# Two stages of a long single-core kernel reordered: the S5 state loop and the pair loop of the sparse attention

## The chip, the cores and the metric

One core of one Trainium2 chip runs the whole program. The time is the device time in microseconds (us); the kernel before took 1408.51 us (median of 3 runs, 1407.64 to 1408.97).

## The reference

The program computes two blocks of a transformer-like network for 256 tokens and width 1024, in float32. The first has two layers of a hybrid mixer and a cross attention. The second has two layers, each a SwiGLU, a mixer and another SwiGLU. The mixer of its first layer is S5, that of its second is sparse attention. Only these two are touched here. Cut to what matters:

```python
def _s5_mixer(u, ...):                     # 64 groups of 16 channels, 64 complex states each
    bu_re, bu_im = einsum(ug, bb_re), einsum(ug, bb_im)
    x_re, x_im = associative_scan(combine, (la_re, la_im, bu_re, bu_im))   # x_t = a x_{t-1} + bu_t
    y = einsum(x_re, c_re) - einsum(x_im, c_im) + d_skip * ug
    y = gelu(y); return y * sigmoid(y @ w_glu)

def _nsa_mixer(u, kv, w_qg, q_norm, w_o, rel_bias):     # 16 heads, 4 key groups
    o_cmp = compressed branch (15 blocks of keys), o_slc = selected branch, o_win = window branch
    # at 256 tokens every block is selected, so slc and win are two dense causal softmaxes
    o = gates[..., 0:1] * o_cmp + gates[..., 1:2] * o_slc + gates[..., 2:3] * o_win
    return o.reshape(bsz, seq, D_MODEL) @ w_o
```

## The kernel before, in words

Nearly all the work is matrix products of weights that are streamed from memory once. Each unit of weights (128 x 1024) is loaded by SP into one of six slots (`RING = 6`), split by ACT into a high part (`hi_parts`, L332) and by DVE into a low part (`lo_parts`, L340), and TensorE (PE) then runs three products per tile (L392 to L394). Each engine follows one list written out by hand, and engines wait for each other by named semaphore values (`when(label)`). PSUM's eight banks go round in three pools, A (0 to 3), S (4, 5) and T (6, 7).

**The S5 core** (`pe_s5` L2281, `act_s5` L2375, `dve_s5` L2454, `pool_s5` L1967, `sp_s5` L2544) handles 1024 channels in eight groups q. The tokens are first rearranged by 32 transfers inside SBUF (`move_u`, 16 for each half a), issued by SP, ACT and POOL. Then, for each q:
- PE `drive(q)`: 32 small products (L2308) that give the input of the scan; `direct(q)`: 4 products (L2328) that start the output bank.
- DVE `products(q)`: two multiplications from PSUM (L2482), an addition and a subtraction (L2490, L2491), two scans (L2497), and one scaling `scale_u4(q+4)` (L2469) while q is below 4.
- POOL multiplies the scanned state by cosines (`s5.p{q}.0`) and sines (`s5.p{q}.1`, both L2063) and subtracts one from the other (`s5.x{q}`, L2066). For q = 7 DVE does this (`dve_last_state`, L2079 and L2082).
- PE multiplies three results into the output bank, 4 products each (L2340), and marks `s5.y{q}`. ACT copies the bank (L2411), PE turns it (`y_turn`, L2318), ACT applies GELU and makes the high part (`act_y`, L2364, L2367), DVE makes the low part (`dve_y_lo`, L2087), and PE turns two groups back for later (`pe_y_nat`, L2357).

The weights `glu` follow. Their units 0 to 3 go into slots that the S5 core uses until late: SP waits for `s5.direct3`, `s5.p6.1`, `s5.direct7` and `s5.p7.1` before it loads units 0, 2, 1 and 3.

**The pair loop** of the sparse attention takes 16 pairs p: two blocks of 128 queries, and in each eight pairs of heads. Pairs 0 to 7 have 128 keys, pairs 8 to 15 have 256. Each pair is two jobs j = 2p and 2p+1 (selected and window branch). The steps of a pair:
- PE scores (L2866) into both banks of pool S; DVE adds the bias and takes the maximum (L2901), which frees the banks; ACT exponentials with sums (L2912); DVE reciprocal (`dve_pair_sum`, L2928); POOL multiplies gate and probabilities (L2937, L2940);
- PE turns the probabilities (`pe_pair_turn`, L2877, pool T); ACT or DVE copies them back (`pair_copy`, L2923; `copied_by_act(j)` says who); PE multiplies with the values (L2887), one pair later.

The scores run `PAIRS_AHEAD = 2` pairs ahead of the turns. Other steps are put between pairs by the dictionaries `between`: conversions of the next weights (L332, L340) and the compressed branch: scores on PE (L3010), bias, maximum and subtraction on DVE (L3142, L3146, L3148), exponential on ACT (L3073), sum, reciprocal, gate and scaling on DVE (L3159 to L3165), turn (L3020) and product (L3032) on PE.

Of the kernel before, what the change touches and what calls it, by code (L numbers as in the profile page):

```python
# [16 lines left out]
P = 128  # L17
# [104 lines left out]
def build(nc, book, d, out, bias_rows):  # L122
    ctx = ExitStack()
    done, when = book.done, book.when
    with ctx:
# [1841 lines left out]
        def pool_s5(pool):  # L1967
# [81 lines left out]
            move_u(pool, 1, U_MOVES[12:16], "s5v")  # L2049
            pool.wait_ge(*when("s5.bu1"))  # L2050
            for q in (0, 1, 3):
                nc.gpsimd.memset(by_sin[q][:, 0, :, 0:1], 0.0).then_inc(*done("s5_pool", f"s5.s0{q}"))
            for q in range(KT - 1):
# [5 lines left out]
                if q == 3:  # L2059
                    pool.wait_ge(*when("s5.bu3"))  # L2060
                for i, (o, tab) in enumerate(((c, s5_cos), (s, s5_sin))):
                    w = bc(tab[:, q].rearrange("p (a c) -> p a c", a=4)[:, :, 0:NC4 - 1], 1, 2)
                    nc.gpsimd.tensor_tensor(o[:, :, :, 1:NC4], z, w, ALU.mult).then_inc(*done("s5_pool", f"s5.p{q}.{i}"))  # L2063
                pool.wait_ge(*when(f"s5.p{q}.0"))
                pool.wait_ge(*when(f"s5.p{q}.1"))
                nc.gpsimd.tensor_tensor(c[:, 0, :, 1:NC4], c[:, 0, :, 1:NC4], s[:, 1, :, 1:NC4], ALU.subtract  # L2066
                                        ).then_inc(*done("s5_pool", f"s5.x{q}"))
            pool.wait_ge(*when(f"s5.x{KT - 1}"))

        def dve_last_state(dve):  # L2070
# [9 lines left out]
            dve.wait_ge(*when(f"s5.p{q}.0"))  # L2080
            dve.wait_ge(*when(f"s5.p{q}.1"))
            nc.vector.tensor_tensor(c[:, 0, :, 1:NC4], c[:, 0, :, 1:NC4], s[:, 1, :, 1:NC4], ALU.subtract  # L2082
                                    ).then_inc(*done("s5_dve", f"s5.x{q}"))
# [197 lines left out]
        def pe_s5(pe):  # L2281
# [42 lines left out]
            for q in range(KT):  # L2324
                b = ahead if q == 1 else take(pe, "A", f"s5.yb{q}")
# [4 lines left out]
                last.then_inc(*done("s5_pe", f"s5.direct{q}"))  # L2330
                if q + 2 < KT:
# [15 lines left out]
            y_turn(KT - 1)  # L2347
            pe_chunk(pe, "glu.0", lifted="s5", after={7: lambda: pe_y_nat(pe, 3)})
# [26 lines left out]
        def act_s5(act):  # L2375
# [27 lines left out]
            move_u(act, 1, U_MOVES[4:12])  # L2403
            sines(3)
            for q in range(KT):
                if q == KT - 1:
# [7 lines left out]
                if q >= 4 and q % 2 == 0:  # L2414
                    act_y_nat(act, q // 2 - 2)
            hi_parts(act, chunk_start("glu.0") + 3)
            act_y(act, KT - 1)
# [36 lines left out]
        def dve_s5(dve):  # L2454
# [32 lines left out]
            for q in range(KT):  # L2487
# [46 lines left out]
        U_DONE = ((16 * 7, 16 * 9), (16 * 12, 16 * 4))  # L2534
# [65 lines left out]
        def pool_kv(pool):  # L2600
# [5 lines left out]
            pool.wait_ge(*when(f"s5.x{KT - 1}"))  # L2606
# [720 lines left out]
```

## Time and profile before

| | |
|---|---|
| median of 3 runs | 1408.51 us |
| the profiled execution | 1408.01 us |
| its span | 1406.0 us |
| PE busy | 1359.8 us (97%) |
| DVE busy | 831.9 us (59%) |
| ACT busy | 797.1 us (57%) |
| POOL busy | 341.8 us (24%) |

The span is from the first to the last instruction of the profile; the execution's own time is 2.01 us longer. Matmuls overlap each other, so PE counts as busy even where a product takes long. In the two stages that are changed PE is not always busy, and these are some 35 us (the S5 core) and 64 us (the pair loop) of the span.

### The profile page before, as it was taken

The page shows a single profiled execution, that of the slowest core. Times are in us where ns is not written, and L with a number is a line of the kernel's source. Part 1 is how long each engine was busy: PE and PEld are TensorE (multiplying, and loading weights), DVE is VectorE, ACT ScalarE, POOL GpSimd, SP SyncE. Part 2 cuts the span into 40 slices and gives each one's busy share as a digit, 9 for nine tenths or more (in the row PEclk, how much of TensorE's full clock was granted, in tenths as well). Part 3 has the DMA queues.
Part 4 walks back from the last instruction along what each step waited for, and adds up shares of the span by engine and source line. Part 5 has one row for each costly group of instructions (what it writes and reads, how often), then busy time and mean ns, then how long its engine had stood idle before and what let it go on. Part 6 is the DMA issues. An engine that isn't in the chain of part 4 may idle for free.

```text
span 1406.0 us, 22406 instructions
## 1 busy us (share of the span) xinstructions
PE 1359.8 (97%) x7511; PEld 1130.2 (80%) x7511; DVE 831.9 (59%) x1344; ACT 797.1 (57%) x1318; POOL 341.8 (24%) x398
## 2 busy tenths in 40 slices
PE   7999999999999999989999999999999978999998
PEld 6888878898777888868788888888888856888887
DVE  6547665457667566657755555645555686555553
ACT  7768476585665454555744445765444566554442
POOL 2011000013349999968200000010000045000000
PEclk9999999999999999999999999999999999999999
DMA  9541635631567554324866664686565401476561
GB/s 336 192 134 42 229 111 160 187 102 45 193 135 225 180 164 153 103 61 139 263 212 182 191 193 145 187 167 221 181 191 185 137 31 46 135 225 193 180 194 45
DMA packets 170863, 224.75 MB, mean 160 GB/s; under 512 B 14864, under 2 KB 114272, under 8 KB 170784
## 3 DMA queue, kind: packets, MB, share of 16 engines
q1 hardware_dynamic: 167888, 217.18, 49.2%
q0 software_dynamic: 2320, 6.18, 2.5%
q8 instruction: 48, 0.79, 0.2%
q10 hardware_dynamic: 576, 0.35, 0.1%
q14 instruction: 31, 0.25, 0.1%
HBM read 221.16 MB, written 1.44 MB: 158 GB/s over the span
## 4 chain that ended last, share of the span: by engine, by line
PE 47%; DVE 3%; ACT 2%; POOL 2%; issue 1%; DMA 1%; ACTq 0%; POOLq 0%; SPq 0%; DVEq 0%
PE psum L1638 12%; PE psum L1626 9%; PE psum L1628 8%; PE psum L1627 8%; PE psum L392 2%; PE psum L394 2%; PE psum L393 2%; PE psum L1665 1%; ACT w_hi L332 1%; DVE w_lo L340 1%; PE psum L2684 1%; POOL arena L2063 1%; DVE arena L2901 1%; PE psum L418 1%; PE psum L2877 0%
## 5 line engine op out<-in xcount | busy, mean ns | idle before, releaser
L1844 DVE TENSOR_TENSOR w_lo<-w_raw,w_hi 128x1024 fp32r<-128x1024 f32 x216 | 281.0, 1304 | 273.4 <-ACT w_hi L1764 273.1
L1764 ACT ACTIVATE w_hi<-w_raw 128x1024 fp32r<-128x1024 f32 x216 | 228.7, 1060 | 306.7 <-PE psum L1628 217.2
L340 DVE TENSOR_TENSOR w_lo<-w_raw,w_hi 128x1024 fp32r<-128x1024 f32 (+5 forms) x191 | 230.1, 1230 | 118.2 <-ACT w_hi L332 117.0
L1626 PE MATMUL psum<-w_hi,x_hi 128*128 128x512 f32 x704 | 280.1, 398 | 1.3 <-ACT arena L2770 0.5
L1628 PE MATMUL psum<-w_hi,x_lo 128*128 128x512 f32 x704 | 274.9, 390 | 0.0
L1627 PE MATMUL psum<-w_lo,x_hi 128*128 128x512 f32 x704 | 274.2, 389 | 0.0
L332 ACT ACTIVATE w_hi<-w_raw 128x1024 fp32r<-128x1024 f32 (+5 forms) x191 | 192.7, 1038 | 99.8 <-PE psum L394 56.7
L392 PE MATMUL psum<-w_hi,x_hi 128*128 128x512 f32 (+6 forms) x608 | 230.3, 379 | 2.1 <-DVE w_lo L340 1.4
L394 PE MATMUL psum<-w_hi,x_lo 128*128 128x512 f32 (+6 forms) x608 | 225.5, 371 | 0.0
L393 PE MATMUL psum<-w_lo,x_hi 128*128 128x512 f32 (+6 forms) x608 | 225.1, 370 | 0.0
L1626 PEld LDWEIGHTS psum<-w_hi,x_hi 128*128 128x128 f32 x704 | 132.3, 188 | 28.6 <-issue 1.5
L1628 PEld LDWEIGHTS psum<-w_hi,x_lo 128*128 128x128 f32 x704 | 132.1, 188 | 28.4
L1627 PEld LDWEIGHTS psum<-w_lo,x_hi 128*128 128x128 f32 x704 | 132.4, 188 | 25.8
L392 PEld LDWEIGHTS psum<-w_hi,x_hi 128*128 128x128 f32 x608 | 114.3, 188 | 22.0 <-DVE w_lo L340 1.4
L394 PEld LDWEIGHTS psum<-w_hi,x_lo 128*128 128x128 f32 x608 | 114.3, 188 | 19.4
L393 PEld LDWEIGHTS psum<-w_lo,x_hi 128*128 128x128 f32 x608 | 114.4, 188 | 17.4
L1638 PE MATMUL psum<-w_hi,f_hi 128*128 128x512 f32 x320 | 99.8, 393 | 1.2 <-DVE f_lo L1838 1.2
L1638 PE MATMUL psum<-w_lo,f_hi 128*128 128x512 f32 x320 | 98.6, 389 | 0.0
L1638 PE MATMUL psum<-w_hi,f_lo 128*128 128x512 f32 x320 | 98.6, 389 | 0.0
L1638 PEld LDWEIGHTS psum<-w_hi,f_lo 128*128 128x128 f32 x320 | 60.1, 188 | 12.6
L1638 PEld LDWEIGHTS psum<-w_lo,f_hi 128*128 128x128 f32 x320 | 60.1, 188 | 12.6
L1638 PEld LDWEIGHTS psum<-w_hi,f_hi 128*128 128x128 f32 x320 | 59.0, 188 | 13.3 <-issue 1.8
(436 smaller groups left out, 1712.0 us busy)
## 6 DMA issues: line engine op xcount, KB each, us to landing
w_raw<-in_ffn_w_in SPq DMA_DIRECT2D x352, 256.0 KB, 3.2
w_raw<-in_ffn_w_out SPq DMA_DIRECT2D x176, 256.0 KB, 2.9
w_raw<-in_w_in SPq DMA_DIRECT2D x88, 256.0 KB, 3.4
w_raw<-in_w_out SPq DMA_DIRECT2D x32, 256.0 KB, 3.7
w_raw<-in_w_kv SPq DMA_DIRECT2D x24, 256.0 KB, 2.9
w_raw<-in_mem_wk SPq DMA_DIRECT2D x16, 256.0 KB, 5.1
w_raw<-in_mem_wv SPq DMA_DIRECT2D x16, 256.0 KB, 5.1
w_raw<-in_mem_wq SPq DMA_DIRECT2D x16, 256.0 KB, 6.3
```

Of the source, the lines that this page charges most:

```text
L332: nc.scalar.activation(w_hi[:, s, 0:size(u)], w_raw[:, s, 0:size(u)], ACT.Copy).then_inc(hi_ready, 1)
L340: nc.vector.tensor_tensor(w_lo[:, s, 0:size(u)], w_raw[:, s, 0:size(u)], w_hi[:, s, 0:size(u)].bitcast(F32), ALU.subtract).then_inc(lo_rea ...
L392: nc.tensor.matmul(o, xh, whi, start=(k + i == x_first), stop=False)
L393: nc.tensor.matmul(o, xh, wlo, start=False, stop=False)
L394: last = nc.tensor.matmul(o, xl, whi, start=False, stop=(k + i == x_first + kts - 1))
L418: last = nc.tensor.transpose(psum[:, b, (2 * c + t) * P:(2 * c + t + 1) * P], src(t, 2 * f + c), ident[:])
L1626: nc.tensor.matmul(o, xh, whi, start=(kt == 0), stop=False)
L1627: nc.tensor.matmul(o, xh, wlo, start=False, stop=False)
L1628: last = nc.tensor.matmul(o, xl, whi, start=False, stop=(kt == KT - 1))
L1638: last = nc.tensor.matmul(psum[:, FF_ACC[2 * t + n], :], x, w[:, n * 512:(n + 1) * 512], start=(first and w is whi and x is xh), stop=Fals ...
L1764: nc.scalar.activation(w_hi[:, s, :], w_raw[:, s, :], ACT.Copy).then_inc(hi_ready, 1)
L1844: nc.vector.tensor_tensor(w_lo[:, s, :], w_raw[:, s, :], w_hi[:, s, :].bitcast(F32), ALU.subtract).then_inc(lo_ready, 1)
```

## The change

In S5:
- the second half's transfers are split 5, 5 and 6 between SP, ACT and POOL instead of 4, 8 and 4, and SP loads glu units 4 and 5 only when all transfers have landed;
- the subtraction `s5.x{q}` is gone. ACT negates the sine product's imaginary part (`s5.n{q}`), and PE multiplies four results into the bank, not three;
- `direct(q+1)` is issued in group q, ahead of that group's state products;
- on DVE the scalings of the second half move one group later (q = 1 to 4), and `dve_y_lo` runs twice in each of groups 5 and 6 instead of once in each of groups 4 and 5;
- the last `y_turn` moves into the first glu chunk, after two of its eight steps; ACT's order of `hi_parts` and `act_y(7)` changes with it.

In the pair loop:
- `PAIRS_AHEAD` is 3;
- the compressed scores are issued as two halves of 64 columns of weights, and one pair earlier (2 and 3 instead of 3 and 4);
- the compressed subtraction and the last scaling go to POOL, between jobs;
- conversions and compressed steps have other places in DVE's and ACT's lists, and ACT copies more of the turned jobs.

```diff
-            for q in (0, 1, 3):
-                nc.gpsimd.memset(by_sin[q][:, 0, :, 0:1], 0.0).then_inc(*done("s5_pool", f"s5.s0{q}"))
+            for q in range(2):
+                nc.gpsimd.memset(by_sin[q][:, :, :, 0:1], 0.0).then_inc(*done("s5_pool", f"s5.s0{q}"))
...
-                pool.wait_ge(*when(f"s5.p{q}.0"))
-                pool.wait_ge(*when(f"s5.p{q}.1"))
-                nc.gpsimd.tensor_tensor(c[:, 0, :, 1:NC4], c[:, 0, :, 1:NC4], s[:, 1, :, 1:NC4], ALU.subtract
-                                        ).then_inc(*done("s5_pool", f"s5.x{q}"))
-            pool.wait_ge(*when(f"s5.x{KT - 1}"))
+            pool.wait_ge(*when(f"s5.p{KT - 1}.1"))
...
+            ahead = direct(0)
+            for q in range(KT):
+                y = ahead
                 if q + 2 < KT:
                     drive(q + 2)
-                if q == 0:
-                    ahead = take(pe, "A", "s5.yb1")
-                    pe_busy(pe, ahead, 4)
-                for label, x, i in ((f"s5.p{q}.0", by_cos[q % 2][:, 1], 1), (f"s5.p{q}.1", by_sin[q][:, 0], 1),
-                                    (f"s5.x{q}", by_cos[q % 2][:, 0], 0)):
-                    pe.wait_ge(*when(label))
+                if q + 1 < KT:
+                    ahead = direct(q + 1)
+                c, s = by_cos[q % 2], by_sin[q]
+                for label, x, i in ((f"s5.p{q}.0", c[:, 1], 1), (None, c[:, 0], 0), (f"s5.p{q}.1", s[:, 0], 1), (f"s5.n{q}", s[:, 1], 0)):
+                    if label:
+                        pe.wait_ge(*when(label))
                     for j in BY_HALF:
                         last = nc.tensor.matmul(y[j // 2][:, :, j % 2, :], x[:, j, :], s5_D[:, 4 * q + j, i, :],
-                                                start=False, stop=(i == 0), skip_group_check=True)
+                                                start=False, stop=(label == f"s5.n{q}"), skip_group_check=True)
                 last.then_inc(*done("s5_pe", f"s5.y{q}"))
                 if q >= 1:
                     y_turn(q - 1)
                 if q % 2 and q >= 3:
                     pe_y_nat(pe, q // 2 - 1)
-            y_turn(KT - 1)
-            pe_chunk(pe, "glu.0", lifted="s5", after={7: lambda: pe_y_nat(pe, 3)})
+            pe_chunk(pe, "glu.0", lifted="s5", after={2: lambda: y_turn(KT - 1), 7: lambda: pe_y_nat(pe, 3)})
...
-            move_u(act, 1, U_MOVES[4:12])
+            move_u(act, 1, U_MOVES[5:10])
             sines(3)
             for q in range(KT):
+                act.wait_ge(*when(f"s5.p{q}.1"))
+                nc.scalar.activation(by_sin[q][:, 1], by_sin[q][:, 1], ACT.Copy, scale=-1.0).then_inc(*done("s5_act", f"s5.n{q}"))
                 if q == KT - 1:
...
-                if q < 4:
-                    scale_u4(q + 4)
-                elif q < 6:
-                    dve_y_lo(dve, q - 4)
+                if 1 <= q <= 4:
+                    scale_u4(q + 3)
+                elif 5 <= q <= 6:
+                    dve_y_lo(dve, 2 * q - 10)
+                    dve_y_lo(dve, 2 * q - 9)
             dve_last_state(dve)
-            for k in (2, 3, 4, 5):
+            lo_parts(dve, chunk_start("glu.0") + 1)
+            for k in (4, 5):
                 dve_y_lo(dve, k)
-            lo_parts(dve, chunk_start("glu.0") + 1)
+            lo_parts(dve, chunk_start("glu.0") + 2)
...
-        U_DONE = ((16 * 7, 16 * 9), (16 * 12, 16 * 4))
+        U_DONE = ((16 * 7, 16 * 9), (16 * 10, 16 * 6))
...
-            return j % 2 == 0 and (p % 2 == 0 if PAIRS[p][0] == 0 else p not in (10, 13))
+            return j % 2 == 0 and p not in (1, 10, 13)
...
+        def pool_compressed(pool, t, scaled):
+            n = n_blocks(t)
+            x = xc[:, t, :, 0:n]
+            pool.wait_ge(*when(("cmp.late" if t == 0 else "cmp.g1") if scaled else f"cmp.max{t}"))
+            nc.gpsimd.tensor_tensor(x, x, bc(cm[:, 2 * t], 2, n), ALU.mult if scaled else ALU.subtract
+                                    ).then_inc(*done("cmp_pool", f"cmp.p{t}" if scaled else f"cmp.sub{t}"))
+
+        def pool_pairs(pool, between):
 
             pool.wait_ge(*when("nsa.gate1"))
             for j in range(2 * len(PAIRS)):
+                if j in between:
+                    pool_compressed(pool, *between[j])
...
-        PAIRS_AHEAD = 2
+        PAIRS_AHEAD = 3
...
             for j in range(2 * m - 1):
+                if j == 2:
+                    dve_pair_max(dve, 2)
                 dve_pair_sum(dve, j)
             for p in range(n):
                 if p in between:
                     between[p]()
                 if p + m < n:
                     dve_pair_max(dve, p + m)
-                if p + 1 < n:
-                    dve_pair_sum(dve, 2 * p + 3)
+                if p + m - 1 < n:
+                    dve_pair_sum(dve, 2 * (p + m) - 1)
...
+                    for x in range(2):
+                        o = psum[HD * x:HD * x + HD, b, 32 * a:32 * a + 32].rearrange("p (i c) -> p i c", i=2)
+                        last = nc.tensor.matmul(o[:, :, 0:n_blocks(t)], qT[:, a, t * P + HD * x:t * P + HD * x + HD],
+                                                kcTz[:, :, NCMP * (a // 2):NCMP * (a // 2) + n_blocks(t)], start=True, stop=True)
...
-            pe_pairs(pe, o_banks, between={3: lambda: compressed_scores(0), 4: lambda: compressed_scores(1), 7: compressed_turn, 8: compressed_out},
-                     first=[lambda: heads([2]), lambda: heads([3], busy={3: 3})])
+            pe_pairs(pe, o_banks, between={2: lambda: compressed_scores(0), 3: lambda: compressed_scores(1), 7: compressed_turn, 8: compressed_out},
+                     first=[lambda: heads([2]), lambda: heads([3], busy={3: 3}), lambda: None])
...
-            act_pairs(act, between={1: convert_to(1), 2: convert_to(2), 4: lambda: compressed_exp(0), 5: lambda: compressed_exp(1),
+            act_pairs(act, between={3: lambda: compressed_exp(0), 4: lambda: compressed_exp(1),
...
-            dve_pairs(dve, between={2: convert_to(1), 3: convert_to(2), 4: lambda: compressed_max(0), 5: lambda: compressed_max(1),
-                                    6: lambda: compressed_scaled(0), 7: lambda: compressed_scaled(1), 9: convert_to(3),
+            dve_pairs(dve, between={1: convert_to(1), 2: lambda: compressed_max(0), 3: lambda: compressed_max(1),
+                                    5: lambda: compressed_scaled(0), 6: lambda: compressed_scaled(1), 7: convert_to(2), 9: convert_to(3),
...
+            pool_pairs(pool, between={11: (0, False), 13: (1, False), 16: (0, True), 18: (1, True)})
```

## Rows read from the trace of the kernel before

**Rows 1.** Windows view: length, busy per engine (count), PE clock, DMA share, GB/s
```profile
1129.00:1193.40 64.40, 52.37 (x435) 36.02 (x435) 48.17 (x216) 41.37 (x154) 35.05 (x64) 0.97 0.14 42
619.50:654.50 35.00, 31.72 (x661) 28.18 (x660) 32.96 (x63) 16.73 (x36) 26.16 (x31) 1.00 0.27 81
...
1132.00:1136.00 4.00, 3.33 (x13) 2.52 (x14) 2.47 (x21) 3.71 (x18) 0.73 (x2) 0.74 0.02 4
```

**Rows 2.** Chain that ended last, S5 stretch: start, us, what
```profile
625.26 1.53 DVE w_raw L2469
...
633.46 1.42 POOL arena L2063
...
635.04 0.69 POOL f_silu L2066
...
651.58 4.55 DMA w_raw<-in_s_w_glu
```

**Rows 3.** Timeline, ACT in S5: start, us, engine, line, operation, idle before
```profile
617.27 4.75 ACTq L2541 DMA_DIRECT2D w_raw<-w_raw  x7
...
628.66 0.41 ACT L2398 ACTIVATE arena<-arena 128x252 f32<-128x252 f32 x1
```

**Rows 4.** Timeline, DVE in S5
```profile
632.59 0.68 DVE L2482 TENSOR_TENSOR psum<-psum,arena 128x512 f32<-128x512 f32 x1
633.19 0.55 DVE L2469 TENSOR_TENSOR w_raw<-w_raw,arena 128x256 f32<-128x256 f32 x1
...
636.08 0.68 DVE L2482 TENSOR_TENSOR psum<-psum,arena 128x512 f32<-128x512 f32 x1
...
649.25 0.84 DVE L2079 TENSOR_TENSOR f_hid<-w_raw,arena 128x504 f32<-128x504 f32 x1
```

**Rows 5.** Timeline, PE in S5 and at the start of glu
```profile
640.33 0.66 PE L2357 MATMUL psum<-ident,arena 128*128 128x128 f32 x4
...
643.65 0.63 PE L2318 MATMUL psum<-ident,arena 128*64 128x64 f32 x16
644.11 0.61 PE L2328 MATMUL psum<-arena,w_raw 128*64 128x128 f32 x8
644.55 1.10 PE L2308 MATMUL psum<-w_raw,arena 128*64 128x64 f32 x32
...
654.56 0.47 PE L392 MATMUL psum<-w_hi,x_hi 128*128 128x512 f32 x1 [0.41 <-DVE w_lo L340]
...
658.52 0.50 PE L392 MATMUL psum<-w_hi,x_hi 128*128 128x512 f32 x1 [0.98 <-DVE w_lo L340]
```

**Rows 6.** Line view of L2234: ns min/median/max, first and last start
```profile
L2234 DVE SCALAR_TENSOR_TENSOR arena<-soft,gain,arena x8: 238/832/1285, 504.1 to 551.3; 128x32 f32<-128x32 f32 x8
```

**Rows 7.** Waits view of PE, pair loop: who waits for whom, us, times, longest
```profile
PE psum L2866 <- DVE arena L2928: 3.6, 5, 1.6
PE psum L2877 <- ACT arena L2923: 2.4, 3, 1.1
PE psum L2866 <- DVE arena L2901: 2.4, 1, 2.4
PE psum L2877 <- POOL arena L2940: 1.5, 1, 1.5
```

**Rows 8.** Timeline, PE in the pair loop
```profile
1144.11 1.96 PE L3010 MATMUL psum<-arena 128*128 128x14 f32 x16
...
1174.64 1.13 PE L2866 MATMUL psum<-arena 64*128 64x512 f32 x4
1175.70 1.09 PE L2877 MATMUL psum<-ident,arena 128*128 128x128 f32 x8
1176.72 1.09 PE L2887 MATMUL psum<-arena 128*64 128x128 f32 x16
1177.75 1.13 PE L2866 MATMUL psum<-arena 64*128 64x512 f32 x4
```

**Rows 9.** Timeline, DVE in the pair loop
```profile
1179.34 1.77 DVE L340 TENSOR_TENSOR w_lo<-w_raw,w_hi 128x1024 fp32r<-128x1024 f32 x1 [1.32 <-ACT w_hi L332]
```

More of the change, by code:

```diff
@@ L2048, in pool_s5 @@
             nc.gpsimd.memset(coef, 0.0).then_inc(*done("s5_pool", "s5.coef0"))
-            move_u(pool, 1, U_MOVES[12:16], "s5v")
+            move_u(pool, 1, U_MOVES[10:16], "s5v")
             pool.wait_ge(*when("s5.bu1"))
-            for q in (0, 1, 3):
-                nc.gpsimd.memset(by_sin[q][:, 0, :, 0:1], 0.0).then_inc(*done("s5_pool", f"s5.s0{q}"))
+            for q in range(2):
+                nc.gpsimd.memset(by_sin[q][:, :, :, 0:1], 0.0).then_inc(*done("s5_pool", f"s5.s0{q}"))
             for q in range(KT - 1):
@@ L2060, in pool_s5 @@
                     pool.wait_ge(*when("s5.bu3"))
+                    nc.gpsimd.memset(by_sin[q][:, 1, :, 0:1], 0.0).then_inc(*done("s5_pool", "s5.s03"))
                 for i, (o, tab) in enumerate(((c, s5_cos), (s, s5_sin))):
@@ L2079, in dve_last_state @@
                 nc.vector.tensor_tensor(o[:, :, :, 1:NC4], z, w, ALU.mult).then_inc(*done("s5_dve", f"s5.p{q}.{i}"))
[L2080 to L2083, printed above, removed]
         def dve_y_lo(dve, k):
@@ L2323, in pe_s5, with direct @@
                 drive(q)
-            for q in range(KT):
-                b = ahead if q == 1 else take(pe, "A", f"s5.yb{q}")
+            def direct(q):
+                b = take(pe, "A", f"s5.yb{q}")
+                if q == 1:
+                    pe_busy(pe, b, 4)
                 y = [psum[NC4 * x:NC4 * x + NC4, b, 0:256].rearrange("p (r a k) -> p r a k", r=L4, a=2) for x in range(2)]
@@ L2415, in act_s5 @@
                     act_y_nat(act, q // 2 - 2)
+            hi_parts(act, chunk_start("glu.0") + 2)
+            act_y(act, KT - 1)
             hi_parts(act, chunk_start("glu.0") + 3)
-            act_y(act, KT - 1)
             act_y_nat(act, 2)
@@ L2546, in sp_s5 @@
             for a in range(2):
-                move_u(sp, a, U_MOVES[0:(5, 4)[a]])
+                move_u(sp, a, U_MOVES[0:5])
             first = chunk_start("glu.0")
@@ L2552, in sp_s5 @@
                 sp.wait_ge(loads[f"s5v{a}"], U_DONE[a][1])
-                sp_units(sp, first + 4 + a, first + 5 + a)
+            sp_units(sp, first + 4, first + 6)
             for u, x in ((0, "s5.direct3"), (2, "s5.p6.1"), (1, "s5.direct7"), (3, "s5.p7.1")):
@@ L2605, in pool_kv @@
             edges = bucket_edges()
-            pool.wait_ge(*when(f"s5.x{KT - 1}"))
+            pool.wait_ge(*when(f"s5.p{KT - 1}.1"))
             step(nc.gpsimd.memset(bias_r[0:NH, :], NEG), "nsa.bias_mask")
@@ L3008, in compressed_scores @@
                 for a in range(NH // 2):
-                    o = psum[:, b, 32 * a:32 * a + 32].rearrange("p (i c) -> p i c", i=2)
-                    last = nc.tensor.matmul(o[:, :, 0:n_blocks(t)], qT[:, a, t * P:(t + 1) * P],
-                                            kcTz[:, :, NCMP * (a // 2):NCMP * (a // 2) + n_blocks(t)], start=True, stop=True)
+                    for x in range(2):
+                        o = psum[HD * x:HD * x + HD, b, 32 * a:32 * a + 32].rearrange("p (i c) -> p i c", i=2)
+                        last = nc.tensor.matmul(o[:, :, 0:n_blocks(t)], qT[:, a, t * P + HD * x:t * P + HD * x + HD],
+                                                kcTz[:, :, NCMP * (a // 2):NCMP * (a // 2) + n_blocks(t)], start=True, stop=True)
                 last.then_inc(*done("cmp_pe", f"cmp.s{t}"))
@@ L3068, in act_nsa @@
             q_out([3])
+            act_pair_exp(act, 2)
             def compressed_exp(t):
@@ L3245, in _ @@
             pool_kv(pool)
-            pool_pairs(pool)
+            pool_pairs(pool, between={11: (0, False), 13: (1, False), 16: (0, True), 18: (1, True)})
         @block.tensor
```

5 lines of the change are left out of this document (1 added, 4 removed).

## Prediction

> **What bounds the kernel now.** I read the windows view first. PE is the bound nearly everywhere, but not in the two stages that change: in the pair loop it is busy 52.4 of 64.4 us, in the S5 core 31.7 of 35.0 us, while DVE there is busy 33.0 of 35.0 [rows 1]. So the change can win at most some 12 us in the one and 3 us in the other. Elsewhere nothing is touched, and PE runs on, so a shift of either stage's end passes to the end of the kernel.
>
> Then the chain of waits through S5. It runs over the transfers, a scaling on DVE, and then from group to group on POOL (the sine product 1.42, the subtraction 0.69), and at the end over a load of glu weights (4.55) [rows 2]. That names POOL. But the timeline of DVE has the same instruction at 632.59 and 636.08 [rows 4]: a group costs DVE 3.49 us, and it has no gap in it. PE's group is 3.14: turn 0.46, direct products 0.44 (644.11 to 644.55), drive 0.93, and three state products at the price of the direct ones, 1.31 [rows 5]. POOL's 3.5, DVE's 3.49 and PE's 3.14 stand side by side. Taking work from one of them shows the next.
>
> Third, the waits of PE in the pair loop, 12.6 us in all in nine rows, of which the four largest are shown: 3.6 for scores behind DVE, 2.4 for turns behind ACT's copies, 2.4 at the start, 1.5 behind POOL near the end [rows 7].
>
> I work in differences by carrying: each engine takes its list in order, each instruction starts at its predecessor's end or 0.07 us after what it waits for, with the durations of the trace. For the pair loop of before this gives an end at 1192.8, where the trace has 1193.2, so its error is some tenths.
>
> **S5, part by part.**
> *Transfers.* ACT issued seven of its eight in 4.75 us [rows 3]; with three fewer its last goes out 2.0 us sooner. DVE's scaling waited for the last to land, by the durations ahead of it some 0.2 us, and began at 625.26 [rows 2]. The scaling now stands a group later, near 628, so the landing costs nothing even if it came no sooner. That scaling took 1.53 against 0.55 for its like [rows 2, 4], because it met a product that POOL had just begun. Gone: 0.2 of waiting and 1.53; back in group 4: one ordinary scaling, 0.45. Term: -1.2.
> *Low parts in pairs.* DVE makes four low parts in groups 5 and 6, where two stood in 4 and 5: +0.8. The second of each pair is the risk. The first arrives while POOL's first product runs and is let in at its end; POOL's second product is by then waiting too. If POOL goes next, the second low part waits for a whole product. Bounds: 0 (DVE keeps its turn) and 1.4 (the product's row, rows 2); from 1.53 less 0.55 it is 1.0. What decides is who goes next. Of eight small two-input instructions of L2234, issued in two runs of four while POOL multiplied, the median is 832 ns, the shortest 238 and the longest 1285 [rows 6]: most waited, so DVE doesn't keep its turn. I take 1.2 each: +2.4.
> The Trainium skill (SBUF — State Buffer, "SBUF: two separate sides") says that a DVE instruction with two SBUF inputs and a GpSimd instruction exclude each other for the whole instruction, whichever starts first; on who goes next it says nothing. The 1.53 agrees with it.
> *POOL.* Without the subtraction a group is 2.8 us, under DVE's 3.49, so nothing more is won there: DVE is late next.
> *PE.* 32 more products, 0.44 a group: 3.58, and 4.17 where a turn back of 0.59 is added (rows 5: 640.33 to 640.92). That is over DVE's 3.49. From the first state products at 627.5, PE would end group 6 near 649.3, with no drives in its last two groups. Group 7's products are not ready before 649.4 to 651.8, so DVE still ends last, but by little. Cost: 0, bound +0.5. The early direct products cost nothing: they fill PE before its wait.
> *Negation on ACT.* Nearest row 0.41 [rows 3]; with a hop 0.5, behind each sine product. In groups 0 to 6 PE works on the other three results meanwhile. In group 7 it is on the path.
> *The end.* The last scan ended at 649.2, where DVE's own products begin [rows 4], and glu began at 654.56 [rows 5], 5.4 us later. Now: last scan, two products 1.35, negation 0.5, high part of unit 0 1.0, low part 1.2, hops 0.3: 4.3 us. Term: -1.1. The last scan comes at 649.2 - 1.2 + 0.8 + 2.4 = 651.2, glu at 655.5: +0.9.
> *Inside glu.* PE waited 0.98 for unit 1 [rows 5], whose load (4.55) was released by the last direct products. These come a group sooner, over 3.5 us, so the wait goes. Against it the last turn now stands inside (0.46), and unit 2 is split only behind the GELU of group 7: by carrying, PE waits 0.5 for it. These cancel. Term by carrying: 0 to -0.1.
> S5: +0.8. Without the 2.4, carrying gives -1.2.
>
> **Pair loop, part by part.**
> *Compressed scores.* 16 instructions in 1.96 us, each 0.118 [rows 8]; as 32 of 64 columns at the drive's price, 0.93 for 32 [rows 5], they save 0.85 to 0.95 twice. Term: -1.8; bound 0, if halves cost what whole ones do.
> The Trainium skill (TensorEngine Tiling (Array Packing), "Key Properties") says that changing the tiling mode drains the engine, and there is one more change at either side now. Rows 8 have such a change between turns and values: 1.02 us from start to start, no more than for the products alone. By that rule the term would shrink by no more than hundredths.
> *Three ahead.* PE's work in a late pair is 3.1 us (1174.64 to 1177.75, rows 8). The extra pair of lead hides latency of the chain maximum, exponentials, reciprocal, POOL. But PE's waits are mostly not for that chain. Scores need their banks back, and pool S still holds one pair: they wait for the previous maximum, however far ahead. Turns wait for ACT's copy of the job before, which stands behind four exponentials of a later pair in ACT's list. Three ahead changes neither. What it does hide is the last wait, 1.5 for POOL.
> *New waits.* DVE's third maximum now stands ahead of the reciprocals of pair 1, and turn 0 is behind scores 3: by carrying it starts at 1139.2, for before at 1137.5. In pairs 2 and 3 the compressed maximum stands in the same step as PE's compressed scores, a step later before; DVE idles 1.2 and 1.5 us for them, its own maximum is behind it, and PE waits 0.6 and 1.0 for scores 6 and 7. In pair 7 the compressed scaling is on POOL behind jobs 16 and 17 and behind the conversion now in DVE's pair 7: PE waits 1.9 for it, against 1.0 on DVE.
> *Pairs 11 to 13.* DVE waits for ACT's high part (1.32), then needs 1.77 because POOL is in its way [rows 9]; the next maximum, exponentials and ACT's copy come after. In the order of before PE then waits 0.7 and 0.6; now there is no scores step left to fill with, and carrying gives 2.3 ahead of turn 26.
> *Sum.* Carried waits of PE: 12.8 before, 15.1 after, +2.3; work -1.75. The loop ends 0.55 later, at 1193.4 where the same carrying gives 1192.8 for before. With every duration of each group varied by -7 to +15% it stays between -0.3 and +1.2.
>
> **Sum.** +0.8 + 0.55 = +1.35. On the profiled execution, 1408.01 (span 1406.0 and 2.0 around it), this is 1409.4; the median of the runs is 0.5 higher, so 1409.8.
>
> **Rivals.**
> *DVE keeps its turn.* S5 is -1.2, the sum -0.65: 1407.9. For it: in the trace no scaling beside POOL was held for the second time, each stood alone. Against it: rows 6. Chance 0.17.
> *The lead pays.* If DVE's and ACT's lists drift so that three ahead takes up the jitter, PE loses none of the 3.6, 2.4 and 1.5 of rows 7, 7.5 us in all; two thirds of that gone with the 1.8 of the scores, less what S5 adds, is some -6: 1402.5. For it: POOL and ACT have slack there, 35 and 41 of 64 us [rows 1]. Against it: banks and list order, above. Chance 0.2.
> *PE's clock falls in the loop's start.* From 1132 to 1136 the granted clock averages 0.74 [rows 1], after 2.4 us of idling [rows 7]; that is about half the stretch at 1.2 GHz. The changed order idles PE 3.5 us between 1137 and 1144, against 1.8. If it falls again there and stays low for 6 us, of which PE works 4, that is +4 at half speed, together with S5 1413.5. It decides if the gaps of 1.1, 0.6 and 0.7 follow each other closely enough. Against it: the loop's mean clock is 0.97 [rows 1], little of which is lost outside its first 8 us, though PE idles there and later too. Chance 0.18.
> *The change doesn't do what it says:* the loads of unit 1 could still come late, since SP loads unit 2 first and this waits for group 6's sine product. Then 0.98 stays: 1410.8, within the forecast's range.
>
> **How the numbers follow.** Forecast 0.45, the rivals 0.17, 0.2 and 0.18. 0.2% is 2.8 us, about what a measurement of this kernel tells from no change. The forecast and the first rival lie within it but for some tails; the second is faster, the third slower. Faster 0.23, within 0.58, slower 0.19. The likeliest case's own range is 1407.5 to 1412; the whole one 1403.5 to 1413.
>
> **What would show it.** Right: no L2066 in S5; four groups of state products; in groups 5 and 6 one low part (L2087) of over 1 us each; glu beginning 0.5 to 1.2 us later than before relative to the first drive, and its unit-1 wait gone; in the pair loop PE waits of about 15 us, one over 1.5 ahead of the compressed turn and one of about 2 ahead of turn 26; compressed scores of 1.0 us. Wrong: low parts at 0.4 throughout; scores steps at less than 3.3 us spacing in pairs 1 to 7; a granted clock under 1.00 after 1140; or a wait of PE that isn't in this list, above all in glu, where it would mean that the order of loads matters more than I say.

## The result, and the profile after

The changed kernel takes 1416.28 us (median of five runs, 1415.98 to 1423.01) against 1408.97 for the kernel before (1407.64 to 1410.88) beside it: ratio 1.0063, 95% interval 1.0046 to 1.0080. It is 7.3 us slower where I forecast 0.8 us for S5 and 0.55 for the pair loop, 1409.8 in all. The profiled execution (1415.98, span 1414.2) is 8.2 us longer in span than that of before. Between fixed marks of the two traces this splits as follows; each figure is the difference of two start times. h is the sum that runs through the layers; PE turns it (L418) for the next stage. glu.0 and glu.1 are the two halves of the glu weights, ff1 is the SwiGLU behind S5, and wo_nsa are the output weights of the attention.

| stretch | before | after | difference |
|---|---|---|---|
| h's first turn ahead of S5, from the start | 606.74 | 606.12 | -0.6 |
| from there to the first drive | 12.74 | 11.42 | -1.3 |
| first drive to glu.0's first matmul | 35.08 | 35.50 | +0.4 |
| glu.0's first matmul to ff1's first | 25.01 | 31.92 | +6.9 |
| ff1 to the pair loop's first scores | 449.46 | 449.26 | -0.2 |
| pair loop, to wo_nsa's first matmul | 64.31 | 67.33 | +3.0 |
| the rest | 212.66 | 212.65 | 0 |

So almost all of it stands in two places: inside glu, where my term was 0, and in the loop, where it was +0.55. The windows of the kernel after (columns as in [rows 1]) show the loop and the S5 core, the counterparts of [rows 1], and below them the stretches that matter:

```profile
1134.20:1201.60 67.40, 53.66 (x467) 36.41 (x467) 45.63 (x209) 42.15 (x157) 36.70 (x68) 0.92 0.13 40
617.50:652.50 35.00, 33.62 (x709) 31.13 (x708) 32.23 (x59) 19.59 (x44) 22.56 (x27) 1.00 0.33 100
668.00:672.00 4.00, 1.90 (x5) 1.55 (x6) 3.60 (x7) 3.41 (x5) 0.00 (x0) 0.57 0.97 268
672.00:676.00 4.00, 4.00 (x12) 3.14 (x11) 2.08 (x3) 0.35 (x1) 0.00 (x0) 0.57 0.98 295
1156.00:1160.00 4.00, 4.00 (x20) 1.89 (x18) 2.40 (x10) 1.86 (x10) 2.13 (x6) 0.59 0.00 0
1166.00:1170.00 4.00, 2.98 (x16) 2.32 (x18) 1.46 (x9) 2.77 (x11) 3.77 (x8) 0.62 0.41 135
1194.00:1198.00 4.00, 4.00 (x36) 3.34 (x34) 2.84 (x4) 0.60 (x1) 1.04 (x1) 0.57 0.07 8
```

Two things are to be seen. In 668 to 676 PE does half its work, first because it stands still, then because the granted clock is 0.57 (mostly the 1.2 GHz level). And in the loop the clock is 0.92 against 0.97 [rows 1]. It falls three times, not in the loop's start but at 1156, 1166 and 1194. Read in slices of 2 us, the loop of before has 3.4 us at 1.2 GHz, the loop of after some 10.2.

The timeline of PE in glu, after. The first two rows answer to glu's rows in [rows 5]: glu.0 began 35.50 us behind the first drive, and the wait of 0.98 is now one of 0.20. Then the last matmul of glu.0 and the first of glu.1:

```profile
653.04 0.47 PE L392 MATMUL psum<-w_hi,x_hi 128*128 128x512 f32 x1 [0.45 <-ACT x_hi L2366]
...
659.76 0.50 PE L392 MATMUL psum<-w_hi,x_hi 128*128 128x512 f32 x1 [0.20 <-DVE w_lo L340]
...
665.61 0.40 PE L394 MATMUL psum<-w_hi,x_lo 128*128 128x512 f32 x1
670.10 0.77 PE L392 MATMUL psum<-w_hi,x_hi 128*128 128x512 f32 x1 [4.09 <-ACT arena L2432]
670.66 0.63 PE L393 MATMUL psum<-w_lo,x_hi 128*128 128x512 f32 x1
```

ACT at the same time:

```profile
665.15 2.94 ACT L332 ACTIVATE w_hi<-w_raw 128x1024 fp32r<-128x1024 f32 x3
668.11 1.28 ACT L2432 ACT_TABLE_LOAD   x1
669.40 1.08 ACT L2432 ACTIVATE arena<-psum 128x512 f32<-128x512 f32 x2
```

PE waits for the first of the two sigmoids. That is the instruction that reads the sums of glu.0's first tile and frees its PSUM bank. Nothing in glu.1's arithmetic needs it. The code says why it is waited for. Pool A has four banks, handed out in turn. Before, from glu.0 to glu.1 four were taken: two tiles, two tiles. The change puts the last turn between them, which takes a fifth, and glu.1's second tile gets the bank of glu.0's first. glu.1 asks for both banks ahead of its first matmul, and the sigmoid stands in ACT's list behind three conversions and a table load.

DVE in S5, after: the pairs of low parts in groups 5 and 6, each x2:

```profile
640.16 1.94 DVE L2080 TENSOR_TENSOR x_lo<-arena,x_hi 128x256 fp32r<-128x256 f32 x2
...
645.04 1.93 DVE L2080 TENSOR_TENSOR x_lo<-arena,x_hi 128x256 fp32r<-128x256 f32 x2
```

PE in the pair loop, after; the first row answers to the compressed scores of [rows 8], the fourth and the last show scores and transposes at 1.2 GHz (at 2.4 GHz they take 1.13 and 1.09 [rows 8]):

```profile
1147.56 1.11 PE L3026 MATMUL psum<-arena 128*64 128x14 f32 x32
...
1154.29 0.70 PE L2870 MATMUL psum<-arena 64*128 64x256 f32 x4 [0.95 <-DVE arena L2932]
1155.81 0.63 PE L2881 MATMUL psum<-ident,arena 128*128 128x128 f32 x4 [0.82 <-ACT arena L2927]
...
1157.16 2.08 PE L2870 MATMUL psum<-arena 64*128 64x512 f32 x4
...
1192.75 1.06 PE L2881 MATMUL psum<-ident,arena 128*128 128x128 f32 x8 [2.16 <-POOL arena L2950]
1193.74 1.54 PE L2891 MATMUL psum<-arena 128*64 128x128 f32 x16
1195.22 1.97 PE L2881 MATMUL psum<-ident,arena 128*128 128x128 f32 x8
```

And the waits view of PE there, against [rows 7]:

```profile
PE psum L2870 <- DVE arena L2932: 4.2, 7, 1.1
PE psum L2881 <- ACT arena L2927: 3.3, 4, 1.1
PE psum L2870 <- DVE arena L2905: 2.4, 1, 2.4
PE psum L2881 <- POOL arena L2950: 2.2, 1, 2.2
PE psum L3036 <- ACT arena L2916: 1.5, 1, 1.5
```

### The profile page after: what moved, and what is told of

Same layout as the page of the kernel before. It is cut to its first block, busy times and chain, and to the rows that moved or that the text cites. A ratio compares the mean times of both kernels' runs of the same rounds, so it can differ in the third digit from the quotient of the medians.

```text
span 1414.2 us, 22590 instructions
## 1 busy us (share of the span) xinstructions
PE 1365.4 (97%) x7607; PEld 1134.6 (80%) x7607; DVE 830.2 (59%) x1336; ACT 801.6 (57%) x1329; POOL 339.9 (24%) x397
## 4 chain that ended last, share of the span: by engine, by line
PE 86%; DVE 6%; ACT 5%; issue 2%; DMA 1%; SPq 0%; ACTq 0%; POOL 0%; DVEq 0%
PE psum L1638 15%; PE psum L1626 11%; PE psum L1628 11%; PE psum L1627 11%; PE psum L392 8%; PE psum L394 8%; PE psum L393 8%; PE psum L418 2%; DVE w_lo L340 1%; PE psum L1665 1%; ACT w_hi L332 1%; PE psum L2340 1%; ACT arena L462 1%; PE psum L2881 1%; DVE arena L2905 1%
```

## The experiments

**The bank, from both sides.** e1 is the changed kernel with one word changed; e2 is the kernel before with the last turn moved and nothing else.

```diff
 e1, in y_turn(q)
-                b = take(pe, "A", f"s5.ytb{q}")
+                b = take(pe, "S" if q == KT - 1 else "A", f"s5.ytb{q}")
 e2, in the kernel before
-            y_turn(KT - 1)
-            pe_chunk(pe, "glu.0", lifted="s5", after={7: ...})
+            pe_chunk(pe, "glu.0", lifted="s5", after={2: lambda: y_turn(KT - 1), 7: ...})
```

> The changed kernel, with the bank of the last turn (y_turn(7), which the change put inside glu.0) taken from pool S instead of pool A. Bank theory: with five takes of the four A banks from glu.0.t0 to glu.1.t1, glu.1's second tile gets the bank that glu.0's first tile holds until the sigmoid of L2432 has read it; with the turn in pool S the wait of 4.09 us ahead of glu.1's first matmul goes, the clock stays at 2.4 GHz in 668 to 676 (another 2.4 us), and the time is 1416.3 - 6.5 + 0 to 1 = 1410 to 1411 us. Rival (late weight parts: the order of ACT's hi parts, not the bank, holds glu.1): the wait stays and the time is 1416 +- 1.

> The kernel before with only the last turn moved from ahead of glu.0 to behind glu.0's second k tile, its bank still from pool A. Bank theory: glu.1 now waits some 3.5 to 4.5 us for glu.0's sigmoid although nothing else of the change is there, and some of the matmuls behind the wait run at 1.2 GHz: 1409 + 4 to 7 = 1413 to 1416 us. Rival (ACT's order or the late units of the change): no wait in glu.1, 1409 +- 0.5.

e1: 1410.39 us, ratio to before 1.0005 (0.9993 to 1.0018). e2: 1413.45, ratio 1.0033 (1.0020 to 1.0046). In e1 no wait stands ahead of glu.1, and its windows are full; in e2 the wait is there to the hundredth, with the same slow matmuls behind it. Windows of e1, then PE in e2:

```profile
668.00:672.00 4.00, 4.00 (x20) 3.29 (x19) 3.27 (x3) 3.97 (x5) 0.00 (x0) 1.00 1.03 255
672.00:676.00 4.00, 4.00 (x19) 3.34 (x18) 3.55 (x8) 3.84 (x5) 0.00 (x0) 1.00 0.94 289
```
```profile
672.12 0.77 PE L392 MATMUL psum<-w_hi,x_hi 128*128 128x512 f32 x1 [4.09 <-ACT arena L2429]
672.69 0.63 PE L393 MATMUL psum<-w_lo,x_hi 128*128 128x512 f32 x1
```

From glu.0's first matmul to ff1's first, e1 takes 25.55 us, the changed kernel 31.92: the bank cost 6.4 us, 4.1 of standing still and the rest, 2.3, of 1.2 GHz behind it. The rival, that late weight parts hold glu.1, falls: e1 leaves ACT's list and all loads as they were.

**The two parts alone.** e3 is the kernel before with the edits from the pair loop on, e4 with the S5 edits, its last turn's bank from pool S as in e1.

```diff
 e3: of the change, from copied_by_act(j) on, the rest as before
+        PAIRS_AHEAD = 3
 e4: of the change, up to U_DONE, the rest as before, and
+                b = take(pe, "S" if q == KT - 1 else "A", f"s5.ytb{q}")
```

> The kernel before with only the edits from the pair loop on (three pairs ahead, halved compressed scores, its subtraction and product on POOL). Theory A (the lead's own waits: 2.16 ahead of turn 26, 1.45 ahead of the compressed turn, and the clock's falls behind them): the loop takes some 3 us more as in the changed kernel, 1409 + 2.5 to 3.5 = 1411.5 to 1412.5. Theory B (the clock falls in the loop came from what the state of the clock was on arrival, 5 us later): the loop costs what my sum said, +0.5, 1409.5 +- 0.5.

> The kernel before with only the S5 edits, and the bank of the last turn from pool S. If the S5 core is 1.5 us ahead at 664 as in the changed kernel and nothing gives it back: 1407.5 +- 0.5, below both kernels. Rival (the gain before 664 came from the clock's state at 615 to 618 and not from the edits, or is given back in glu.1, whose weights land no earlier): 1409 +- 0.5.

e3: 1411.77 (1409.03 to 1417.08), ratio 1.0028 (1.0015 to 1.0042). e4: 1408.89, ratio 0.9996 (0.9988 to 1.0005). e3's twelve executions lie apart: seven at 1409.0 to 1411.8 with a mean granted clock of 0.993 to 0.996, five at 1415.4 to 1417.1 with 0.988 to 0.990. In four series of the kernel before, 117 executions in all, none has a mean clock under 0.992. So the edits of the loop bring more time at 1.2 GHz in some executions, and the loop's cost isn't one number; it goes with how long the clock is low. The profiled one has two stretches, back to back, where before has one; windows of e3:

```profile
1130.00:1136.00 6.00, 4.26 (x12) 3.00 (x13) 3.44 (x24) 4.88 (x20) 1.06 (x4) 0.60 0.00 0
```

**Filling the waits.** e5 is e1 with matmuls on the identity, whose result nobody reads, ahead of five waits, written to the bank that is used next or to one that is free.

```diff
 e5, in pe_pairs; the same ahead of pairs 3 and 7, compressed turn 1 and turn 26
+                if p == 1:
+                    pe_busy(pe, o_banks[0][1], 9)
                 pe_pair_scores(pe, p)
```

> The changed kernel with the last turn's bank from pool S (1410.4 us) and matmuls on the identity, whose result nobody reads, in five of the pair loop's PE waits: 9 ahead of pair 1's scores (wait 2.35), 4 ahead of pair 3's (1.13), 3 ahead of pair 7's (0.95), 5 ahead of the compressed turn 1 (1.45), 8 ahead of turn 26 (2.16), at 0.24 us each. Clock theory (the loop's extra time is the stretches at 1.2 GHz, three of 3.4 us in its profile against one before, each some 1.3 us, and they come where PE has just stood still): with the waits filled, at most one stretch is left in the loop, the loop takes 64 to 65 us instead of 66.9, and the time is 1408 +- 0.7. Rival (the loop's own order costs it; the clock falls anyway): three stretches stay, 1410.4 to 1411.5.

e5: 1414.37, ratio 1.0034 (1.0021 to 1.0047): slower. My sizes were wrong. The profile counts two instructions for each such matmul, and I had read its price per instruction. Nine took 4.05 us in a wait of 2.35. The eight ahead of turn 26 began only when the bank was free, which was when the product came too, so all 3.72 were lost. Still the loop, at 68.72 us, has no moment at 1.2 GHz, in PE's timeline and in the window:

```profile
1129.47 4.05 PE L368 MATMUL psum<-ident 128*128 128x256 f32 x18
...
1186.29 3.72 PE L368 MATMUL psum<-ident 128*128 128x256 f32 x16 [2.13 <-ACT arena L2929]
```
```profile
1128.30:1197.10 68.80, 61.76 (x525) 44.24 (x525) 44.44 (x209) 42.44 (x157) 36.81 (x68) 1.00 0.13 39
```

e10 is e5 with sizes that fit, e9 the kernel before with four in the wait of 2.35 alone.

```diff
 e9, in the kernel before; in e10 with 4, and 2, 2 and 3 at pairs 3 and 7 and compressed turn 1
+                if p == 1:
+                    pe_busy(pe, o_banks[0][1], 4)
                 pe_pair_scores(pe, p)
```

> The kernel before with four matmuls on the identity (0.45 us each, as e5's profile has them) in PE's wait of 2.35 us ahead of pair 1's scores, and nothing else. If the stretch of 3.4 us at 1.2 GHz at the loop's start comes from PE standing still there, it goes: the scores of pairs 1 and 2 and the turns between run at full rate, the loop takes 64.3 - 1.3 = 63.0 us, and the time is 1.3 below before's. If the clock falls for a reason that lies ahead of the wait, or the fall only moves to the next wait, the loop stays at 64 and the time within 0.5 of before's.

> e5 with the identity matmuls sized by what they really take (0.45 us each; e5 had twice the time of each wait): 4 ahead of pair 1's scores, 2 ahead of pair 3's, 2 ahead of pair 7's, 3 ahead of compressed turn 1, none ahead of turn 26. Clock theory: no stretch at 1.2 GHz before 1190, loop 63.5 to 65 us, 1408.3 +- 0.8 (2 below e1, 6 below e5). If e5 was slow for another reason than its oversize (filling itself slows the neighbours), it stays over 1411.

e10: 1408.78, ratio 0.9998 (0.9988 to 1.0007), loop 64.50, its one stretch at 1186, with no fill near. e9: 1407.65 (1405.60 to 1413.07), ratio 0.9991 (0.9977 to 1.0005). e9's stretch at the loop's start is gone (1132 to 1136 now at 1.00, for 0.74 in [rows 1]), and two came back to back at 1156 to 1163, behind a wait of 1.58 us ahead of scores. So here filling one wait did not keep the clock up in the rest of the loop; the interval doesn't tell e9 from before. e9, windows:

```profile
1132.00:1136.00 4.00, 3.57 (x20) 2.23 (x20) 2.58 (x20) 3.97 (x18) 1.45 (x4) 1.00 0.02 4
1158.00:1162.00 4.00, 4.00 (x17) 1.85 (x15) 1.60 (x10) 2.41 (x10) 2.43 (x4) 0.50 0.00 0
```

**The low parts, and the halved scores.** e6 is e4 with one low part in each of groups 5 and 6 and the other two behind the last state; e7 is e4 with the compressed scores in column halves, in the old loop.

```diff
 e6
-                    dve_y_lo(dve, 2 * q - 10)
-                    dve_y_lo(dve, 2 * q - 9)
+                    dve_y_lo(dve, q - 5)
             dve_last_state(dve)
+            for k in (2, 3):
+                dve_y_lo(dve, k)
 e7, in compressed_scores(t), as in the change
-                    last = nc.tensor.matmul(o[:, :, 0:n_blocks(t)], qT[:, a, t * P:(t + 1) * P],
+                    for x in range(2):
+                        o = psum[HD * x:HD * x + HD, b, 32 * a:32 * a + 32].rearrange(...)
+                        last = nc.tensor.matmul(o[:, :, 0:n_blocks(t)], qT[:, a, t * P + HD * x:t * P + HD * x + HD],
```

> The S5 edits alone with the last turn's bank from pool S (1408.9 us, glu.0's first matmul 34.3 us behind DVE's first rotation), but only one low part in each of groups 5 and 6 and the other two behind the last state, where DVE stands 1.43 us for the weights' hi part. Theory of my forecast (the second low part of a group waits 1.2 us for POOL's product between the two, and DVE's list sets the end): groups 5 and 6 are 1.2 shorter each, glu.0 begins 31.9 to 32.5 behind the first rotation, 1408.9 - 2.0 = 1406.9. Rival (POOL's products and ACT's list set the end, DVE would only stand elsewhere): glu.0 stays at 33.8 to 34.3, 1408.9 +- 0.4.

> The S5 edits alone with the last turn's bank from pool S (1408.9 us) and, in the pair loop of before (two pairs ahead), only the compressed scores in column halves: 1.05 us a block instead of 1.96. Theory (my term of -1.8): the loop goes from 64.35 to 62.8 us, 1407.3. Rival (DVE's list or the softmax of the pairs sets the loop there, PE only waits 0.9 longer behind each block): 1408.9 +- 0.3.

e6: 1409.75, ratio 1.0001 (0.9991 to 1.0010). e7: 1409.78 (1406.54 to 1411.09), ratio 0.9995 (0.9986 to 1.0005). In e6 a low part takes 0.52 us where the pair took 1.94, so the second of a pair did cost 1.4, of which 0.4 is its own work and 1.0 its wait for POOL's product. But glu.0 begins only 0.65 sooner (34.85 behind the first drive, for 35.50): PE now waits for the negation on ACT and for the low part of the weights. DVE, then PE in e6:

```profile
643.58 0.52 DVE L2080 TENSOR_TENSOR x_lo<-arena,x_hi 128x256 fp32r<-128x256 f32 x1
```
```profile
653.14 0.66 PE L2340 MATMUL psum<-arena 128*64 128x128 f32 x8 [0.41 <-ACT arena L2406]
...
655.55 0.47 PE L392 MATMUL psum<-w_hi,x_hi 128*128 128x512 f32 x1 [0.70 <-DVE w_lo L340]
```

In e7 the compressed scores are cheap, and the clock takes the gain back: the profiled loop is 65.34 us with 10.2 at 1.2 GHz, where e4's is 64.35 with 3.4. Its two quickest executions, 1406.54 and 1406.65, are those with the highest mean clock, 0.997. Windows of e7:

```profile
1158.00:1162.00 4.00, 3.00 (x18) 2.10 (x19) 3.41 (x13) 2.39 (x10) 2.12 (x3) 0.60 0.01 4
1162.00:1166.00 4.00, 4.00 (x15) 2.50 (x16) 1.54 (x9) 1.82 (x8) 1.64 (x5) 0.54 0.00 0
```

**Together.** e8 has e6's and e7's edits and oversized fills, e11 the same with sized ones (4, 3, 2 and 1), e12 adds four identity matmuls in S5:

```diff
 e12, in pe_s5
             b = take(pe, "A", "s5.rowb")
-            pe_busy(pe, b, 4)
+            pe_busy(pe, b, 8)
```

> e6 and e7 together with identity matmuls in four waits of the loop (9 ahead of pair 1's scores, 6 ahead of pair 9's, 4 ahead of compressed turn 1, 6 ahead of the last turn). If all three theories hold: 1408.9 - 2.0 - 1.6 - 1.3 = 1404.0 +- 1. If DVE, POOL or ACT set both stages: 1408 to 1409.

> e8 with its identity matmuls at half their number (4 ahead of pair 1's scores, 3 ahead of pair 9's, 2 ahead of compressed turn 1, 1 ahead of the last turn). e8's fills lasted 1.70 + 1.28 + 0.90 + 2.0 = 5.9 us longer than the waits they stood in; with two thirds of that back and no new stretch at 1.2 GHz: loop 62 to 62.5 us, 1406 +- 0.7, the first version below before by more than 0.2%. If the stretches come back (the waits left are still enough): 1408 to 1409.

> e11 with eight instead of four identity matmuls ahead of the S5 row product, in the wait of 2.29 us there. The changed kernel's own profile had no stretch at 1.2 GHz at 614 to 620 and began DVE's first rotation 9.42 us behind h's turn, all others had one and began it 10.9 behind. If the wait brings the fall: 1.5 below e11, 1404.5 +- 0.7. If the fall there hangs on the FFN's end and not on the wait: equal to e11.

e8: 1410.07 (1409.59 to 1410.96), ratio 1.0002 (0.9993 to 1.0011), clock 0.999 in each of eleven executions, loop 66.23 for its fills. e11: 1408.28, ratio 0.9988 (0.9977 to 0.9998); its loop has 10.2 us at 1.2 GHz without a break. e12: 1403.95 (1403.12 to 1404.49), ratio 0.9963 (0.9948 to 0.9977), the quickest of all and quicker than both kernels. Its first drive comes 11.42 us behind h's turn (in e11 13.09), its loop takes 61.84. The forecast of 1404.5 was met in part by luck: I gave the four matmuls 1.5 us, and they brought 4.3 against e11. The other 2.9 lie in the loop (64.74 in e11), whose code is the same in both. All seven executions of e12 have a mean clock of 1.000, e11's twelve 0.995 to 0.999. So whether the clock falls in the loop doesn't hang on the loop's code alone; what it was here that four matmuls some 500 us earlier changed is open. PE, then windows of e12:

```profile
610.39 3.62 PE L368 MATMUL psum<-ident 128*128 128x256 f32 x16
614.58 0.45 PE L2288 MATMUL psum<-arena,gain 128*32 128x32 f32 x16 [0.57 <-DVE arena L2461]
```
```profile
614.00:618.00 4.00, 3.13 (x37) 2.44 (x38) 2.09 (x7) 2.62 (x6) 1.75 (x5) 1.00 0.19 50
1126.80:1188.70 61.90, 54.70 (x487) 36.87 (x487) 48.10 (x216) 41.32 (x154) 34.93 (x64) 1.00 0.15 44
```

**The edits at equal clock.** e13 is the kernel before with e12's fills, e14 adds the S5 edits, e15 the whole change with sized fills.

> The kernel before with the identity matmuls of e12 (eight ahead of the S5 row product, 4, 3, 2 and 1 in the loop) and no other edit, so that all its executions run without a stretch at 1.2 GHz. Clock theory: 1408.8 - 1.5 (S5 row) - 1.3 (the loop's stretch), so 1405.5 to 1406, with a spread under 1.5 us. If e12's gain was mostly the halved scores and the spread low parts: 1407.5 to 1408.5.

> The change's S5 edits, with the last turn's bank from pool S, in the kernel of e13. At equal clock what is left is the edit itself. My forecast's sum (+0.8, with 2.4 for the two pairs of low parts): e13 + 0.8, 1406.3 to 1406.8. Rival (the core is a gain of some 1 us that the clock hid, as e4's ratio of 0.9996 suggests): 0.7 to 1 below e13.

> The whole change, with only the last turn's bank from pool S, and identity matmuls in the row's wait (8) and in the loop's (4, 2, 2, 3). At equal clock the lead of three with halved scores against e14's loop: my sum said +0.55, so 1407 to 1407.4, with no stretch or one at 1188 behind the unfilled wait ahead of turn 26. If the lead really costs the loop 3 us whatever the clock: over 1409.

Medians 1406.83, 1409.66 and 1406.94; ratios to before 0.9986 (0.9975 to 0.9997), 0.9996 (0.9984 to 1.0007) and 0.9984 (0.9975 to 0.9994). The clock still fell in some, so my "no stretch at 1.2 GHz" for e13 was wrong: seven of e14's twelve have a mean of 0.996 and take 1409.6 to 1410.2. Of the executions at 0.999 or 1.000, e13 has eight (1404.54 to 1407.46, median 1405.94), e14 five (1406.62 to 1407.45, median 1406.84) and e15 eight (1405.94 to 1407.18, median 1406.50). By these medians the S5 edits cost some 0.9 us at equal clock, and the new loop against the old gives some 0.3 back: +0.6 in all. But e13's eight fall into two groups, 1404.5 to 1405.2 and 1406.7 to 1407.5, which the clock doesn't tell apart; against the first e14 is 1.9 slower, against the second level. In the profiles h's first turn to ff1's first matmul takes 70.73 in e13, 72.51 in e14, 1.8 more. So the 0.9 is an estimate with 0 to 1.9 around it, and both differences stay well under the 6.9 and 3.0 of the table above. The profiled e13, with 13.7 us in a row at 1.2 GHz where PE has no gap, and e15's loop:

```profile
1142.00:1156.00 14.00, 14.00 (x74) 10.72 (x75) 7.94 (x44) 5.76 (x27) 5.57 (x14) 0.52 0.15 50
```
```profile
1129.60:1192.60 63.00, 54.23 (x489) 37.35 (x489) 45.52 (x209) 42.13 (x157) 36.61 (x68) 1.00 0.14 43
```

## Why the prediction was wrong

**The step that failed** is "Inside glu": "the last turn now stands inside (0.46)", "these cancel", term 0 to -0.1. It was +6.9. Of this the bank is 6.4. I priced the turn by its matmuls and by the loads around it, and didn't count the bank that it takes: PE waited 4.09 us for it and then worked at 1.2 GHz. The carrying knew engines and what they wait for, but PSUM banks only in the pair loop. The waits that I did weigh came out as said: unit 1's 0.98 gone, unit 2's 0.20 for my 0.5. My list of what would prove me wrong had "a wait of PE that isn't in this list, above all in glu", but gave the order of loads as its reason, and e1 shows that this had no part in it. Without the bank the new order still takes 25.5 to 25.6 us from glu.0 to ff1 in all its eleven profiles, where the old one takes 25.0 (before), 24.6 (e3), 24.2 (e13) and 23.9 (e9): 0.5 to 1.7 more than my 0, for which I have no cause.

**S5 up to glu**: forecast +0.9 to glu.0's start relative to the first drive, measured +0.4. The low parts: I took a wait of 1.2 for each second one on top of its own 0.4, and the pairs give 1.0, so 2.0 for my 2.4. What I bounded by [rows 6] alone is thus shown: DVE doesn't keep its turn beside POOL. The Trainium skill (SBUF — State Buffer, "SBUF: two separate sides") has the exclusion and not who goes next; here POOL's second product went between. The 0.4 that the waits came short is nearly all by which the whole did: DVE's last state stands 31.30 us behind the first drive, for 29.77 before, 1.5 later where I said 2.0, and the end took 4.2 for my 4.3. Taking the waits away wins less than they cost: in e6 DVE's last state comes 2.6 us sooner, 28.75, and glu.0 only 0.65, since the end then hangs on ACT's and DVE's lists. And the old order itself isn't fixed. The same S5 code reaches glu.0 at 35.08 and 35.09 in before and e13, and at 33.96, 33.94 and 33.87 in e3, e2 and e9; the new one at 35.46 to 35.52 in eight profiles. What sets the old order's two values I didn't find.

**The pair loop**: each wait that I named came. The compressed scores went from 1.96 to 1.11; ahead of compressed turn 1 PE waits 1.45 (I said 1.9), ahead of turn 26 2.16 (2.3), all waits together 14.4 in the waits view (15.1). For my +0.55, e15 against e14 leaves -0.3 at equal clock, at the edge of my -0.3 to +1.2. But the loop took 3.0 longer, and that is the clock: this is the second step that failed, the loop's sum, which let PE wait longer and held the clock at its old value. The sign "a granted clock under 1.00 after 1140" came. I had a rival for it, with its place and its price wrong: it named 1137 to 1144, and the falls came at 1156, 1166 and 1194, behind 0.95 and 0.82, behind 1.45, and behind 2.16; it asked 4 us for 6 at 1.2 GHz, where the table below gives 1.0 to 1.6 for 3.4. Moreover it isn't one event that comes or doesn't. By the profiled loops, length against time at 1.2 GHz:

| order | 0 us | 3.4 | 6.8 | 10.2 | 13.7 |
|---|---|---|---|---|---|
| new, three ahead | 62.94 (e15) | 64.50 (e10) | 65.94 (e3) | 66.85 (e1), 67.33 (after) | |
| old, two ahead | | 64.31 (before), 64.35 (e4), 64.80 (e2) | 65.56 (e6), 65.39 (e9) | 66.75 (e14) | 67.78 (e13) |
| two ahead, halved scores | 61.84 (e12) | | | 64.74 (e11), 65.34 (e7) | |

(e9 to e15 have waits filled. e5 and e8, at 0 us, are left out, since their fills outlast the waits: 68.72 and 66.23.) Along a row, by the mean of each cell, 3.4 us more at 1.2 GHz go with 1.0 to 1.6 us; in a column, new and old order differ by 0.6 at most. The third row is 1.1 below the first at 0 us: the halved scores alone do better without the lead, whose waits I had at +2.3. So the miss has two causes: a bank that I didn't count, and a clock that I held fixed while PE's waits changed. The first is shown by e1 and e2. For the second, the table and e15 show that the loop's 3 us go with the time at 1.2 GHz, and e3 that the loop's edits bring more of it. Why they do isn't shown: the old order too has 10.2 and 13.7 us in e14 and e13, and e11 and e12 differ with the same loop. Which executions get one stretch and which three is not explained either. The Trainium skill (TensorE: Matmul & The Clock Gate, "A second HAM failure mode: psum-queue depth-cycling") says of another kernel that its PE idles briefly and so often between groups of matmuls that it goes back and forth between its two clocks. The loops of before and after agree, with 3.4 and 10.2 us low behind waits of 0.8 to 2.4.

**The rivals.** "DVE keeps its turn" is refuted by the 1.94. (Its S5 term of -1.2 also doesn't follow from the sum as shown, which gives +0.8 - 2.4 = -1.6.) "The lead pays" is too: the waits for banks and for ACT's copies stayed (4.2 and 3.3 for my 3.6 and 2.4 of [rows 7]), only the last one changed its place. "The change doesn't do what it says" was wrong, its wait went.

## What to carry to other kernels

Where a step that takes a buffer from a rotating pool is moved past others that take from it, write out the takes from there to the next long holder: here five takes of four banks cost 6.4 us, and another pool's idle bank gave it back. In a stage where PE isn't the bound, look at the granted clock before crediting a saving: e7 took twice 0.85 us of work from PE, and its profiled loop came out 1.0 longer, with three times as long at 1.2 GHz. Judge such edits by executions at the same clock, or fill the gaps first, with the length of the filler read from the profile.

## What was not expected of the hardware

- The loops of the seventeen profiles had 0, 3.4, 6.8, 10.2 or 13.7 us at 1.2 GHz, with nearly the same code.
- Once down, the clock stayed so through work without a gap: e13 had PE busy 14.00 of 14 us at a granted 0.52, e14 10.00 of 10 at 0.54 (below). Being busy did not bring it back at once.
- Four more identity matmuls at 612 us took away the fall at 614 to 620 in all four profiles that have them (e12 to e15; first drive at 11.41 or 11.42 us behind h's turn, otherwise 12.7 to 13.1 but for after and e5, which had no fall there either). The price of that fall is 1.3 to 1.7 us.
- Between executions of the same kernel the mean clock went from 0.993 to 0.999 (e9) and the time with it from 1413.07 to 1405.60; e12, at 1.000 in all seven, spread over 1.4 us.

```profile
1144.00:1154.00 10.00, 10.00 (x54) 7.54 (x54) 5.02 (x24) 3.47 (x17) 3.83 (x9) 0.54 0.17 55
```
